# Inverting the recurrence's triangular matrices on 32x32 blocks

## The chip, the cores and the metric

The kernel runs on one core of a Trainium2 chip. The metric is the device time of one execution in microseconds. The engines are TensorE (PE), VectorE (DVE), ScalarE (ACT), GpSimd (POOL) and SyncE (SP), which issues most DMAs. Each runs its own instruction stream in order, and they wait for each other by semaphores.

## What is computed

Two transformer blocks run one after the other over 1024 positions of width 1024 in fp32. The change concerns the second block's recurrent mixer alone: 8 heads of 64, one step per position.

```python
def rwkv7_step(state, inp):
    r_t, w_t, k_t, v_t, a_t, b_t = inp
    sa = jnp.einsum('bhij,bhj->bhi', state, a_t)
    state = state * w_t[:, :, None, :] + sa[..., None] * b_t[:, :, None, :] + v_t[..., None] * k_t[:, :, None, :]
    y = jnp.einsum('bhij,bhj->bhi', state, r_t)
    return state, y
```

The kernel works in chunks of 64 positions. Within a chunk the steps depend on each other through a strictly lower triangular 64x64 matrix M for each head (products of the scaled a and b rows), and the chunk's update needs the inverse of I - M, a lower triangular matrix with ones on its diagonal. Sixteen chunks and eight heads make 128 inverses. Beside the recurrence the second block has a band attention and its projections.

## The kernel before

A "pair-chunk" cp is two neighbouring chunks, 0 to 7 in all; par tells its two chunks apart. Tiles of a pair-chunk hold 8 matrices of 64 columns on each half of the 128 partitions, 16 matrices in 512 columns. The pair-chunks 0 to 3 use data of the first half of the sequence (positions 0 to 511), 4 to 7 of the second.

Order.pre lists a pair-chunk's preparation: pre_x turns v, k and b by matmuls against the identity (L1916); pre_ar, pre_mm and pre_kn are masked products of 64x64 blocks (L1932; masked by DVE at L2808, L2814, L2821); pre_v multiplies KN with v (L1946, evacuated by ACT); pre_i (DVE, L2828 to L2835) and pre_t0 (DVE, L2841) build the first approximations TT and T. Then come five levels. Level l doubles the size of the diagonal blocks that are inverted already, from 2 to 64:

- pre_up: 16 matmuls of 64x64x64 (L1984), AR with T; DVE masks the result with the level's mask lv[l] into X (L2847, two passes of 128x256);
- pre_turn (levels 0 to 3): 16 matmuls (L1999) of TT with X; DVE adds the result to T (L2855, two passes);
- pre_add: 16 matmuls (helper blocks, L1946) of X with TT; DVE adds the result to TT (L2862, two passes).

Order.seq then carries the state through the pair-chunk's two chunks: seq_x (L2011, L2021, L2029), seq_u (L2042), which needs TT of level 4, and seq_z (L2053, L2060). Order.puts_out normalises the outputs (DVE; POOL's seq_gain, L3399 to L3407) and turns them back with seq_out (L2073, DVE L2922). pres, seqs and outs loop over the pair-chunks; pair-chunk cp may start when the outputs of cp - 2 are done, pair-chunk 4 also needs the second half's projections.

The order of all work is written down ahead of time by a planner, Order.flow. It holds a modelled time for each engine and the costs of each step from the function work. Each stream (the gemm tiles as the main one, the pres, seqs, outs, head norms and three lanes of attention bands beside it) offers its next step as soon as its model says that the last one has ended; the gemm fills what is left. So the costs in work decide the order of the instructions on all engines. The eight PSUM banks of P8 are handed out by room; a group of up, turn or add takes two. A gemm product of fp32 takes three matmuls of a 128x512 tile (L1525, L1526, L1527, or L1565 to L1567); DVE and ACT split the weights (L2106, L2967). A band's steps are band_s (L1857; DVE L2699, L2706, L2710; ACT L3271), band_t (transposes at L1511, ACT L3279), band_o (L1878) and band_y (DVE L2716). The gemm stream stops after r1 until pair-chunk 3's operands are read (step ("read", 3), set after pre_kn). After seq_out of pair-chunk 7 and the bands of the first half the gemm fin0 follows, then fin1.

## Time and profile before

| | |
|---|---|
| median of 3 runs | 2421.11 us (2420.31 to 2425.67) |
| the profiled execution | 2418.48 us, of which the span is 2416.6 us |
| mean granted PE clock | 0.972 |
| PE / DVE / ACT / POOL busy | 2277.8 / 1456.7 / 937.6 / 78.7 us |
| instructions in the span | 43216 |

The profile is of one execution. Busy time is the union of an engine's instructions. A matmul in fp32 stands in it as two records, each a weight load (PEld) and a matmul (PE). Matmuls of different tiles of the array overlap, so a group's busy time is shorter than the sum of its matmuls; pages and windows count them with their modelled ends. Times in the timeline are microseconds from the span's start.

### The profile page before, as it was taken

To read this page: it belongs to the slowest core of one execution; us is meant where nothing else is said; L and a number is where in the kernel's file an instruction comes from. 1 tells how busy PE (TensorE), PEld (TensorE's weight loads), DVE (VectorE), ACT (ScalarE), POOL (GpSimd) and SP (SyncE) were. 2 spreads that over 40 slices of the span, in tenths; PEclk is the share of its full clock that TensorE was granted. 3 is DMA by queue.
4 is the path that set the end of the run, shared out by engine and by line. 5 is a ranking of instruction groups with operands and counts; after the bars stand their busy time and mean duration, and the time that the engine had idled before them with its cause. 6 is when DMAs were issued, how large, how long until landed. Compare 5 with 4: busy or idle time off the path is not lost. (4 is left out here: it accounts for less than half of the span.)

```text
span 2416.6 us, 43216 instructions
## 1 busy us (share of the span) xinstructions
PE 2277.8 (94%) x18830; PEld 1848.8 (77%) x18830; DVE 1456.7 (60%) x2456; ACT 937.6 (39%) x1532; POOL 78.7 (3%) x61
## 2 busy tenths in 40 slices
PE   7999988999999999999999999999999998789789
PEld 5777767788888888888878888778777776567667
DVE  5575866565434886777753454646455655767743
ACT  4446432444333443333342433354333232335441
POOL 0000000000000000000000000002000001200000
PEclk9999989999999999999999999989999999799989
DMA  5332252544123232222365534333323113111044
GB/s 179 88 94 66 69 170 71 173 123 129 53 62 119 77 96 83 79 79 86 93 196 164 157 90 135 98 113 110 109 80 107 51 37 97 41 44 44 3 129 150
DMA packets 329349, 238.15 MB, mean 99 GB/s; under 512 B 10948, under 2 KB 288580, under 8 KB 329032
## 3 DMA queue, kind: packets, MB, share of 16 engines
q1 hardware_dynamic: 326424, 229.82, 31.7%
q10 hardware_dynamic: 2736, 5.57, 0.6%
q8 instruction: 148, 2.42, 0.4%
q14 instruction: 41, 0.34, 0.0%
HBM read 202.33 MB, written 33.03 MB: 97 GB/s over the span
## 5 line engine op out<-in xcount | busy, mean ns | idle before, releaser
L1525 PE MATMUL PS<-SR 128*128 128x512 f32 (+2 forms) x1696 | 681.6, 402 | 43.2 <-DVE SR L2106 34.8
L1526 PE MATMUL PS<-SR 128*128 128x512 f32 (+2 forms) x1696 | 659.9, 389 | 0.0
L1527 PE MATMUL PS<-SR 128*128 128x512 f32 (+2 forms) x1696 | 659.7, 389 | 0.0
L2106 DVE TENSOR_TENSOR SR<-SB,SR 128x1024 fp32r<-128x1024 f32 (+1 forms) x240 | 289.1, 1206 | 289.8 <-ACT SR L2967 289.5
L1525 PEld LDWEIGHTS PS<-SR 128*128 128x128 f32 (+1 forms) x1696 | 320.4, 189 | 128.3 <-DVE SR L2106 36.9
L1527 PEld LDWEIGHTS PS<-SR 128*128 128x128 f32 (+1 forms) x1696 | 320.2, 189 | 68.7
L1526 PEld LDWEIGHTS PS<-SR 128*128 128x128 f32 (+1 forms) x1696 | 320.9, 189 | 62.2 <-issue 1.7
L2967 ACT ACTIVATE SR<-SB 128x1024 fp32r<-128x1024 f32 (+1 forms) x240 | 247.5, 1033 | 254.9 <-DMA SB<-in_w_down 116.1
L1546 PE MATMUL PS<-SR 128*128 128x512 f32 x624 | 243.4, 390 | 0.3 <-DVE SR L2232 0.3
L1548 PE MATMUL PS<-SR 128*128 128x512 f32 x624 | 242.8, 389 | 0.0
L1547 PE MATMUL PS<-SR 128*128 128x512 f32 x624 | 242.7, 389 | 0.0
L1546 PEld LDWEIGHTS PS<-SR 128*128 128x128 f32 x624 | 117.1, 188 | 25.1 <-DVE SR L2232 0.7
L1548 PEld LDWEIGHTS PS<-SR 128*128 128x128 f32 x624 | 117.1, 188 | 24.6
L1547 PEld LDWEIGHTS PS<-SR 128*128 128x128 f32 x624 | 117.1, 188 | 24.4 <-issue 0.2
L1511 PE MATMUL PS<-SB 128*128 128x128 f32 (+2 forms) x560 | 87.1, 288 | 31.9 <-DVE SB L2710 13.5
L1511 PEld LDWEIGHTS PS<-SB 128*128 128x128 f32 (+2 forms) x560 | 63.4, 145 | 49.7 <-DVE SB L2710 15.2
L2974 ACT ACTIVATE SB<-PS 128x512 f32<-128x512 f32 (+1 forms) x71 | 39.1, 572 | 151.1 <-PE PS L1527 113.0
L2254 DVE TENSOR_TENSOR SR<-SB,SR 128x1536 fp32r<-128x1536 f32 (+2 forms) x66 | 87.0, 1347 | 0.9 <-ACT SR L3031 0.9
L3031 ACT ACTIVATE SR<-SB 128x1536 fp32r<-128x1536 f32 (+2 forms) x66 | 74.2, 1156 | 20.0 <-DVE SB L2244 18.9
L2142 DVE TENSOR_TENSOR SB<-PS,SB 128x512 f32<-128x512 f32 x48 | 33.2, 691 | 78.7 <-PE PS L1527 78.7
L3279 ACT ACTIVATE SB<-PS 128x640 f32<-128x640 f32 (+4 forms) x64 | 36.4, 569 | 93.7 <-PE PS L1511 93.6
L3065 ACT ACTIVATE SB<-SB 128x1024 f32<-128x1024 f32 x22 | 27.4, 1245 | 116.5 <-DVE SB L2304 116.5
(315 smaller groups left out, 3032.2 us busy)
## 6 DMA issues: line engine op xcount, KB each, us to landing
SB<-in_w_in SPq DMA_DIRECT2D x110, 512.0 KB, 4.0
SB<-in_w_up SPq DMA_DIRECT2D x88, 256.0 KB, 3.3
SB<-in_w_out SPq DMA_DIRECT2D x32, 512.0 KB, 4.2
SB<-in_w_down SPq DMA_DIRECT2D x32, 512.0 KB, 4.1
SB<-in_w_ada SPq DMA_DIRECT2D x12, 1024.0 KB, 5.2
hidden<-SB SPq DMA_DIRECT2D x22, 512.0 KB, 3.4
SB<-hidden SPq DMA_DIRECT2D x43, 256.0 KB, 5.3
asides<-SB SPq DMA_DIRECT2D x36, 256.0 KB, 4.1
```

Of the source, the lines that this page charges most:

```text
L1511: return pe.transpose(out, in_, m.I[0:n, 0:n])
L1525: pe.matmul(out, whi[:, k - k0, :], hi[k], start=(k == 0), stop=False)
L1526: pe.matmul(out, whi[:, k - k0, :], lo[k], start=False, stop=False)
L1527: i = pe.matmul(out, wlo[:, k - k0, :], hi[k], start=False, stop=(k == j.K - 1))
L1546: pe.matmul(out, whi[:, k, :], hi[k], start=first and k == 0, stop=False, skip_group_check=True)
L1547: pe.matmul(out, whi[:, k, :], lo[k], start=False, stop=False, skip_group_check=True)
L1548: x = pe.matmul(out, wlo[:, k, :], hi[k], start=False, stop=(k == 3), skip_group_check=True)
L2106: v.tensor_tensor(m.f32r(a, kn * cn), m.f32(a, kn * cn), m.f32r(a + 1024, kn * cn).bitcast(F32), SUB).then_inc(*on("split.v", p))
L2254: v.tensor_tensor(m.up_unit(m.SR, p, a, 0, b - a), f32_of(p, a, b - a), m.up_unit(m.SR, p, a, 1, b - a).bitcast(F32), SUB).then_inc(*on("u ...
L2967: a.activation(m.f32r(at_ + 1024, kn * cn), m.f32(at_, kn * cn), ACT.Copy).then_inc(*on("split.a", p))
L2974: a.activation(j.dst(t), src, j.func, scale=j.scale).then_inc(*on("gemm.a", "ev", j.name, t))
L3031: a.activation(m.up_unit(m.SR, p, lo, 1, hi - lo), m.up_unit(m.SB, p, lo, 0, hi - lo), ACT.Copy).then_inc(*on("up.a", "hi", p, g))
```

## The change

Only the diagonal blocks of 32x32 are inverted by levels, four in place of five, on compact tiles: TB holds T and TT of all blocks (Tc and TTc, 256 columns each, one set for all pair-chunks), Xc the X. A group of up, turn or add is 32 matmuls of 32x32x32, one on each diagonal 32x32 tile of the array in turn, into one PSUM bank, with one DVE pass of 128x256 behind it. pre_mm computes the diagonal blocks of M and of its transpose (64 matmuls with 64 rows and 32 columns), and DVE masks them and adds the identity in one further pass, which gives T and TT of level -1; pre_i and pre_t0 go. At the end level 4 computes the lower left 32x32 block: up of M's lower left block with T (32 matmuls), a copy to Xc, add with TT (16 matmuls), and copies of the result by DVE (partitions 64 to 95) and ACT (partitions 0 to 31) into the full TT. ACT copies the diagonal blocks into TT (pre_own, four activations), POOL clears TT at the start of each pair-chunk (pre_zero). seq_u waits for the three writers. The costs in work are set anew, the masks become 32 wide, and norms_qk(1) is planned after "qk0".

```diff
-        self.m2, M = f32(X0 + 6656, 640), f32(X0 + 7296, 512)
+        self.m2, TB = f32(X0 + 6656, 352), f32(X0 + 7296, 512)
...
+        self.m0 = v3(m2[:, 128:192], 2).unsqueeze(2).to_broadcast([128, 2, 4, 32])
+        *self.lv, self.I32 = (m2[:, 192 + 32 * i:224 + 32 * i] for i in range(5))
+        self.TB, self.Xc = TB, work(27904, 256)
+        by_kind = TB.rearrange("p (a q j t) -> p a q j t", a=2, q=2, j=4)
+        self.Tc, self.TTc = by_kind[:, :, 0], by_kind[:, :, 1]
...
-        "pre_x": [("pe", 1.0), ("a", 1.0)], "pre_ar": [("pe", 0.95), ("v", 1.38)], "pre_mm": [("pe", 0.48), ("v", 0.84)],
-        "pre_kn": [("pe", 0.95), ("v", 1.38)], "pre_i": [("v", 2.2)], "pre_v": [("pe", 1.9), ("a", 1.2)],
-        "pre_t0": [("v", 0.7)], "pre_up": [("pe", 0.67), ("v", 0.84)], "pre_add": [("pe", 0.95), ("v", 0.84)],
-        "pre_turn": [("pe", 0.67), ("v", 0.84)], "seq_x": [("pe", 1.7), ("v", 0.42)], "seq_u": [("pe", 0.58), ("a", 0.4)],
+        "pre_x": [("pe", 1.0), ("a", 1.0)], "pre_ar": [("pe", 0.95), ("v", 1.38)], "pre_mm": [("pe", 0.6), ("v", 1.55)],
+        "pre_kn": [("pe", 0.95), ("v", 1.38)], "pre_own": [("a", 1.4)], "pre_v": [("pe", 1.9), ("a", 1.2)],
+        "pre_up": [("pe", 0.5), ("v", 0.45)], "pre_add": [("pe", 0.5), ("v", 0.45)], "pre_turn": [("pe", 0.5), ("v", 0.45)], "seq_x": [("pe", 1.7), ("v", 0.42)], "seq_u": [("pe", 0.58), ("a", 0.4)],
...
-                if step[0] not in ("pre_x", "pre_add", "pre_i"):
+                if step[0] not in ("pre_x", "pre_own") and (step[0] != "pre_add" or step[2] == 4):
...
-        yield [("pre_i", cp)]
         yield from one(("pre_v", cp), "pre.a", "nv", cp)
-        yield [("pre_t0", cp)]
-        for l in range(5):
-            yield from one(("pre_up", cp, l), "pre.v", "X", cp, l)
-            if l < 4:
-                yield from one(("pre_turn", cp, l), "pre.v", "T", cp, l)
-            yield from one(("pre_add", cp, l), "pre.v", "TT", cp, l)
+        for l in range(4):
+            yield from single(("pre_up", cp, l), ("pre.v", "X", cp, l))
+            yield from single(("pre_turn", cp, l), ("pre.v", "T", cp, l))
+            yield from single(("pre_add", cp, l), ("pre.v", "TT", cp, l))
+        yield [("pre_own", cp)]
+        yield from single(("pre_up", cp, 4), ("pre.v", "X", cp, 4))
+        yield from single(("pre_add", cp, 4), ("pre.v", "TT", cp, 4), ("pre.a", "far", cp))
         self.done.add(("pre", cp))
...
-                  self.seqs(), self.pres(), self.outs(), self.rotated(1), self.lora_of(1), self.norms_qk(1),
+                  self.seqs(), self.pres(), self.outs(), self.rotated(1), self.lora_of(1), chain(self.after("qk0"), self.norms_qk(1)),
...
+    def corners():
+
+        return [(par, j, h, d, slice(64 * h + 32 * d, 64 * h + 32 * d + 32)) for j in range(4) for par in range(2) for h in range(2)
+                for d in range(2)]
...
+        for q, (lhs, rhs) in enumerate(((sg, aa), (aa, sg))):
+            for j in range(4):
+                for d in range(2):
+                    for par in range(2):
+                        sl = slice(128 * (cp % 4) + 64 * par + 32 * d, 128 * (cp % 4) + 64 * par + 32 * d + 32)
+                        for a in range(2):
+                            to = 64 * (par ^ a) + 32 * d
+                            x = pe.matmul(bank(got[par][0])[to:to + 32, 128 * q + 32 * j:128 * q + 32 * j + 32], lhs[j][half(a), sl],
+                                          rhs[j][half(a), sl], start=True, stop=True)
...
+    def pre_up(cp, l, b, free):
+        AR = m.per[cp % 2]["AR"]
+        w.wait_ge(*at("pre.v", "ar", cp, 1))
+        w.wait_ge(*(at("pre.v", "T", cp, l - 1) if l else at("pre.v", "T", cp)))
+        out = corner(b, free)
+        for par, j, h, d, ps in corners():
+            d, to = (1 - d, slice(64 * h + 32 - 32 * d, 64 * h + 64 - 32 * d)) if l == 4 else (d, ps)
+            c = 512 * par + 64 * j + 32 * d
+            x = pe.matmul(out(to, par, j), AR[ps, c:c + 32], m.Tc[ps, par, j], start=True, stop=True)
         x.then_inc(*on("pre.pe", "up", cp, l))
...
+    def pre_turn(cp, l, b, free):
+        w.wait_ge(*at("pre.v", "X", cp, l))
+        w.wait_ge(*at("pre.v", "TT", cp, l - 1))
+        out = corner(b, free)
+        for par, j, h, d, ps in corners():
+            x = pe.matmul(out(ps, par, j), m.TTc[ps, par, j], Xc(ps, par, j), start=True, stop=True)
         x.then_inc(*on("pre.pe", "turn", cp, l))
+
+    def pre_add(cp, l, b, free):
+        w.wait_ge(*at("pre.v", "X", cp, l))
+        w.wait_ge(*at("pre.v", "TT", cp, l - 1))
+        out = corner(b, free)
+        for par, j, h, d, ps in corners():
+            if l < 4 or d:
+                x = pe.matmul(out(slice(64 * h, 64 * h + 32) if l == 4 else ps, par, j), Xc(ps, par, j), m.TTc[ps, par, j], start=True,
+                              stop=True)
+        x.then_inc(*on("pre.pe", "add", cp, l))
...
-        w.wait_ge(*at("pre.v", "TT", cp, 4, 1))
+        w.wait_ge(*at("pre.v", "TT", cp, 4))
+        w.wait_ge(*at("pre.a", "far", cp))
+        w.wait_ge(*at("pre.a", "own", cp))
...
+        if cp >= 1:
+            w.wait_ge(*at("pre.a", "own", cp - 1))
         for a in range(2):
-            v.tensor_tensor(heads(m.per[cp % 2]["M"], a), h4(bank(got[a][0])[:, 0:256]), bc(m.m0), MUL).then_inc(
-                *on("pre.v", "mm", cp, a))
+            v.tensor_tensor(m.TB[:, 256 * a:256 * a + 256].rearrange("p (q j t) -> p q j t", q=2, j=4),
+                            bank(got[a][0])[:, 0:256].rearrange("p (q j t) -> p q j t", q=2, j=4), m.m0, MUL).then_inc(*on("pre.v", "mm", cp, a))
+        w.wait_ge(*at("pre.v", "mm", cp, 1))
+        v.tensor_tensor(v3(m.TB, 16), v3(m.TB, 16), m.I32.unsqueeze(1).to_broadcast([128, 16, 32]), ADD).then_inc(*on("pre.v", "T", cp))
+        S.also("pre.v", "TT", cp, -1)
...
         w.wait_ge(*at("pre.pe", "up", cp, l))
-        w.wait_ge(*(at("pre.pe", "add", cp, l - 1) if l else at("pre.pe", "v", cp)))
-        for f in range(2):
-            v.tensor_tensor(side(m.per[cp % 2]["KN"][:, 512:1024], f), side4(bank(got[f][0])),
-                            m.lv[l].unsqueeze(1).unsqueeze(1).to_broadcast([128, 2, 2, 64]), MUL).then_inc(*on("pre.v", "X", cp, l, f))
-
-    def pre_turn(cp, l, got):
+        w.wait_ge(*(at("pre.pe", "add", cp, l - 1) if l else at("pre.pe", "mm", cp)))
+        if l < 4:
+            v.tensor_tensor(h8(m.Xc), h8(bank(b)[:, 0:256]), m.lv[l].unsqueeze(1).to_broadcast([128, 8, 32]), MUL).then_inc(
+                *on("pre.v", "X", cp, l))
+        else:
+            v.tensor_copy(m.Xc, bank(b)[:, 0:256]).then_inc(*on("pre.v", "X", cp, l))
...
+        w.wait_ge(*(at("pre.v", "T", cp, l - 1) if l else at("pre.v", "T", cp)))
+        v.tensor_tensor(m.Tc, corner(b), m.Tc, ADD).then_inc(*on("pre.v", "T", cp, l))
...
+        if l < 4:
+            v.tensor_tensor(m.TTc, corner(b), m.TTc, ADD).then_inc(*on("pre.v", "TT", cp, l))
+        else:
+            w.wait_ge(*at("pre.g", "zero", cp))
+            v.tensor_copy(h8(m.per[cp % 2]["TT"])[64:96, :, 32:64], h8(bank(b)[:, 0:256])[64:96]).then_inc(*on("pre.v", "TT", cp, l))
...
+    def pre_own(cp):
+        w.wait_ge(*at("pre.v", "TT", cp, 3))
+        w.wait_ge(*at("pre.g", "zero", cp))
+        TT = m.per[cp % 2]["TT"].rearrange("p (a j t) -> p a j t", a=2, j=4)
+        for h in range(2):
+            for d in range(2):
+                ps = slice(64 * h + 32 * d, 64 * h + 32 * d + 32)
+                i = a.activation(TT[ps, :, :, 32 * d:32 * d + 32], m.TTc[ps], ACT.Copy)
+        i.then_inc(*on("pre.a", "own", cp))
+
+    def pre_add(cp, l, b, free):
+        if l == 4:
+            w.wait_ge(*at("pre.pe", "add", cp, 4))
+            w.wait_ge(*at("pre.g", "zero", cp))
+            a.activation(h8(m.per[cp % 2]["TT"])[0:32, :, 32:64], h8(bank(b)[:, 0:256])[0:32], ACT.Copy).then_inc(*on("pre.a", "far", cp))
...
+    def pre_zero(cp):
+        if cp > 1:
+            w.wait_ge(*at("seq.v", "yr", cp - 2))
+            w.wait_ge(*at("seq.pe", "y", cp - 2, 1))
...
+        g.memset(m.per[cp % 2]["TT"], 0.0).then_inc(*on("pre.g", "zero", cp))
```

## Rows read from the trace of the kernel before

**Rows 1.** The page, part 1: busy us, share of the span, instructions.
```profile
PE 2277.8 (94%) x18830; PEld 1848.8 (77%) x18830; DVE 1456.7 (60%) x2456; ACT 937.6 (39%) x1532; POOL 78.7 (3%) x61
```

**Rows 2.** Windows: stretch, length, busy (count) PE, PEld, DVE, ACT, POOL; PE clock, DMA share, GB/s.
```profile
1700.00:1911.50 211.50, 210.68 (x3089) 164.31 (x3087) 114.51 (x220) 67.47 (x100) 10.24 (x8) 0.99 0.30 91
1911.50:1937.00 25.50, 18.64 (x740) 16.54 (x739) 14.39 (x38) 3.38 (x8) 0.00 (x0) 1.00 0.09 25
...
2040.00:2080.00 40.00, 18.77 (x88) 12.44 (x92) 28.59 (x57) 15.14 (x35) 17.54 (x11) 0.56 0.37 125
2080.00:2290.00 210.00, 181.93 (x4664) 146.02 (x4658) 148.64 (x424) 87.90 (x199) 14.15 (x12) 0.96 0.08 27
2290.00:2318.00 28.00, 11.59 (x95) 7.85 (x92) 18.59 (x40) 16.83 (x29) 4.46 (x4) 0.69 0.25 63
```

**Rows 3.** Groups by line: operands, count | busy us, mean ns | idle before, releaser.
```profile
L1946 PEld LDWEIGHTS PS<-SB 64*64 64x64 f32 x1792 | 56.7, 136 | 15.8 <-issue 9.1 <-DVE SB L2847 3.5 <-DVE SB L2821 2.5
L2862 DVE TENSOR_TENSOR SB<-PS,SB 128x256 f32<-128x256 f32 x80 | 30.1, 419 | 25.9 <-PE PS L1946 25.6
L2847 DVE TENSOR_TENSOR SB<-PS,SB 128x256 f32<-128x256 f32 x80 | 29.9, 416 | 11.3 <-PE PS L1984 11.3
L2855 DVE TENSOR_TENSOR SB<-PS,SB 128x256 f32<-128x256 f32 x64 | 24.1, 418 | 21.0 <-PE PS L1999 21.0
L2832 DVE TENSOR_TENSOR SB<-SB 64x128 f32<-64x128 f32 x32 | 7.8, 283 | 0.2
L2841 DVE TENSOR_TENSOR SB<-SB 128x512 f32<-128x512 f32 x8 | 6.4, 798 | 0.0
L2835 DVE TENSOR_TENSOR SB<-SB 128x512 f32<-128x512 f32 x8 | 5.5, 692 | 0.3
L2828 DVE TENSOR_TENSOR SB<-SB 128x256 f32<-128x256 f32 x8 | 3.4, 419 | 0.0
```

**Rows 4.** Timeline: start us, us, engine line operation, count; groups within the gemm stream.
```profile
1745.00 1.01 PEld L1946 LDWEIGHTS PS<-SB 64*64 64x64 f32 x32 [0.36 <-issue]
...
1746.08 0.50 PE L1525 MATMUL PS<-SR 128*128 128x512 f32 x1
...
1747.66 0.56 PEld L1984 LDWEIGHTS PS<-SB 64*64 64x64 f32 x32 [0.36 <-issue]
...
1748.29 0.50 PE L1842 MATMUL PS<-SR 36*128 36x512 f32 x1
```

**Rows 5.** Timeline: one level without cover, from 1914 us.
```profile
1914.24 0.69 PE L1984 MATMUL PS<-SB 64*64 64x64 f32 x32 [0.88 <-DVE SB L2855]
1915.01 0.76 DVE L2847 TENSOR_TENSOR SB<-PS,SB 128x256 f32<-128x256 f32 x2 [0.16 <-PE PS L1984]
...
1915.82 0.69 PE L1999 MATMUL PS<-SB 64*64 64x64 f32 x32 [0.89 <-DVE SB L2847]
...
1917.40 0.69 PE L1984 MATMUL PS<-SB 64*64 64x64 f32 x32
```

**Rows 6.** Groups on two tiles: 128 columns (group by line, timeline), and one bank.
```profile
L1672 PE MATMUL PS<-SB 128*64 128x128 f32 x240 | 17.4, 289 | 0.0
...
320.96 1.09 PE L1672 MATMUL PS<-SB 128*64 128x128 f32 x16
...
1924.15 0.54 PEld L2011 LDWEIGHTS PS<-SB 64*64 64x64 f32 x16
```

**Rows 7.** Chain of waits from 2150 to 2230: shares of its 80 us by line.
```profile
by line: PE PS L1946 10.6%; PE PS L1857 10.1%; PE PS L1878 8.3%; DVE SB L2710 7.7%; PE PS L1511 7.0%; issue 6.8%; DVE SB L2699 5.5%; PE PS L1999 3.9%; PE PS L1984 3.7%; DVE SB L2847 2.5%; DVE SB L2862 2.5%; PE PS L1916 2.4%; DVE SB L2855 1.
```

**Rows 8.** Groups by line: the nearest rows for ACT's and POOL's new steps.
```profile
L3342 ACT ACTIVATE SB<-PS 128x256 f32<-128x256 f32 x16 | 6.1, 384 | 56.9 <-PE PS L2042 56.9
...
L3404 POOL TENSOR_TENSOR SB<-SB 128x512 f32<-128x512 f32 x8 | 8.7, 1093 | 0.0
```

**Rows 9.** Timeline: pre_v and the first up of pair-chunk 6.
```profile
2191.81 2.08 PE L1946 MATMUL PS<-SB 64*64 64x64 f32 x64 [0.71 <-DVE SB L2821]
...
2196.59 0.69 PE L1984 MATMUL PS<-SB 64*64 64x64 f32 x32 [0.76 <-DVE SB L2841]
```

## What the change does to the time, predicted

> **What bounds the kernel now.** I read the page first, then the windows of the last 700 us, then single stretches of the timeline and of the chain of waits. The page shows TensorE (PE) at 94% and VectorE (DVE) at 60% of the span [rows 1], so an edit pays where PE has less to do or stops waiting. All the code that changes runs between 1700 and 2290 us. The windows split that time into three stages with different limits [rows 2].
>
> Stage A, 1700 to 2040: the four pair-chunks of the first half are prepared between gemm tiles. PE is full (210.68 of 211.5 us), so here only PE time counts, apart from 1911.5 to 1937. There the gemm stream has run out until pair-chunk 3 has been read, and PE works 18.64 of 25.5 us: 6.9 us of idling.
>
> Stage B, 2040 to 2080, PE clock 0.56: projection preparation and a transfer. No edited step runs in it, and I cost it at nothing.
>
> Stage C, 2080 to 2318: pair-chunks 4 to 7 beside the attention bands. PE works 181.93 of 210 us up to 2290 and 11.59 of 28 after, DVE 148.64 and 18.59. Neither is full. Each level of the inverse alternates PE, DVE, PE, DVE, and the last output of pair-chunk 7 opens the final gemm. The chain of waits from 2150 to 2230 goes mostly through PE, 10.6% of it through L1946 alone, the rest of the inverse through L1984 3.7%, L1999 3.9%, and DVE's L2847 and L2862 2.5% each [rows 7].
>
> **The price of a group of small matmuls.** The trace shows each fp32 matmul as two records, weights plus matmul. A group of up or turn has 16 matmuls, 32 records, spread over all four 64x64 tiles of the array; an add (L1946) has as many, but its order leaves only two tiles alternating. Weight loads take 0.56 us in the up group and 1.01 us in the add [rows 4]. Less one load of 0.136 us [rows 3], over 31 steps, that is 13.7 to 13.9 ns and 28.4 ns per record: 55 to 57 ns per record and tile both times. So it is the tile that sets the pace. From its start to the next gemm matmul the up group takes 1747.66 to 1748.29, 0.63 us, and the add 1745.00 to 1746.08, 1.08 us: 31 steps and a fixed 0.20 us.
>
> How does the tile's time depend on the moving columns? A group of 16 records with 128 columns on two tiles takes 1.09 us [rows 6]; less one matmul of 0.289 us, over 15 steps, 53 ns, or 107 ns per record and tile. From 107 at 128 columns and 57 at 64 a line gives about 32 ns at 32 columns. No row has 32 columns: the bounds are 28 (half of 57) and 57 (no gain). I take 31.6, on the line. The new groups of up, turn and add go round four diagonal tiles, so 7.9 ns per record (bounds 7 and 13.9).
>
> **Part by part, per pair-chunk, eight of them.**
> PE: up and turn become 32 matmuls of 32 columns, 64 records: 63 x 7.9 ns + 0.20 = 0.70 us against 0.63, nine times, +0.6. The first four adds cost 0.70 against 1.08, -1.5; the last add (32 records on two tiles, 31 x 15.8 ns + 0.20) 0.69, -0.4. The masked product pre_mm goes from 32 to 128 records over eight tiles; between 3.9 ns (tile) and 7.9 ns I take 6, so 0.96 against 0.63, +0.3. Sum: -1.0 us. The groups stay as many as they were.
> DVE: 28 passes of 128x256 become 14, two of which are now copies. The old ones cost 30.1 + 29.9 + 24.1 = 84.1 us for all eight [rows 3]; half goes, -42 us. pre_i (L2828, L2832, L2835) and pre_t0 (L2841) go: 3.4 + 7.8 + 5.5 + 6.4 = 23.1 us. pre_mm keeps its two passes and gains one of 128x512 at 0.69 us, +5.5. Sum -60 us, 7.4 per pair-chunk. The copy of 32 partitions costs what a full pass costs, as pieces on 64 partitions cost 283 ns for 128 columns; bounds 0.1 and 0.42.
> ACT gains four copies of the diagonal blocks and one of the far block, 256 elements per partition each; nearest row 384 ns [rows 8]: 1.9 us. They stand after level 3, beside up, X and add of the last level (about 2.3 us), and in front of Us in ACT's queue. ACT is busy 87.90 of 210 us in stage C [rows 2]; cover gone, the price is up to 1.9 us per pair-chunk, bound 0 to 8 us in stage C.
> POOL gains a memset of TT. Bounds 0.3 and 1.4 us (a 128x512 pass takes 1.09 [rows 8]). It waits for the output of two pair-chunks before; behind it in the queue is the next gain step, which waits for DVE later still. TT is needed only after level 3, some 20 us on: nothing on the path. The load g_load beside it does not move.
> New waits: DVE's pre_mm waits for ACT's own of the pair-chunk before, as TB is shared, and behind it queue pre_kn and the bands' passes; own is done long before, since seq_u already needed it. seq_u waits for three events in place of one; the last level ends about when it did. The order by planner is cast anew by the shorter costs, which also lets a group take one PSUM bank in place of two; norms_qk(1) is only held behind its first half. I give these nothing, -5 to +5 us.
>
> **The sum.** Stage A: PE -1.0 x 4 = -3.9 us. The 6.9 us of idling end when pair-chunk 3 is read. A level without cover takes 1914.24 to 1915.82 to 1917.40, 3.16 us [rows 5]; each half is 0.77 from the group's start to DVE's, 0.76 of DVE and 0.05 to the next group. The new level takes 2 x (0.84 + 0.42 + 0.05), 2.6 us. Three pair-chunks of five levels are 8 us shorter bare, and pre_i and pre_t0 lie no longer ahead of the first up; that is more than 6.9, so I take all of it. Stage A: -10.8 us.
> Stage C: the chain of 80 us has 8.5 us in L1946; 0.38 of 1.08 goes, -3.0. L2847, L2862 and L2855 hold some 4.8 us, of which 0.34 of 0.76 goes, -2.2; up and turn +0.6. That is -4.6 in 80 us, -13 over 230. The front: after pre_v (2191.81 + 2.08) the first up waits until 2196.59, the last 0.76 us of it for pre_t0 [rows 9], the rest covered by bands; between 0.8 and 2.7 per pair-chunk I take 2, -8. pre_mm: +0.5 per pair-chunk, +2. Stage C: -19 us.
> Together -30 us. The profiled execution has a span of 2416.6 and a time of 2418.48 us; its forecast is 2388.5. The median of the runs lies 2.6 us above it, so the forecast for the median is 2391 us.
>
> **A page against it.** The rows show the tile's time following the columns from 128 to 64 [rows 4, 6]. The Trainium skill, TensorEngine Tiling (Array Packing), Instruction Overhead, says that every matmul bears about 60 cycles, so that 60 columns cost no less than one, and warns not to take a tiling factor from a dimension that is already small. By it the records would double at the old pace, which is the second rival below; by the line they do not. No row here is below 64 columns, so the trace leaves it open.
>
> **Rivals.**
> 1. The stage C gain isn't there: the bands' own chain (score, maximum, exponential, turn, output) sets the end, and shorter levels only open gaps. For it: bands hold PE L1857, L1878 and L1511, each as large on the chain as L1946. Against it: the inverse is in the chain all along, and seq_out of pair-chunk 7 precedes the final gemm while bands are still left to run beside it. Then stage A's 10.8 and at most a third of stage C's: 2404 to 2414, about 2409.
> 2. The other side: the pace stays per record. A nanosecond more per record costs PE 0.95 us per pair-chunk: 3.8 us in stage A, and 2.5 in stage C at two thirds on the path, 6.3 in all. The gain of 30 is used up at 7.9 + 4.8 = 12.7 ns. At 13.9 ns, the shortest pace of the rows, it is +8 us: 2429 (2421 to 2437). For it: no row shows less. Against it: two tiles and four tiles give the same time per tile.
> 3. Four row groups writing into one PSUM bank take turns. Old groups use two banks, new ones one. Price 31.6 ns per record: +24 x 6.3, about 2540. Against it: L2011 writes one bank from two tiles, 16 records in 0.54 us, 27 ns apart, the pace of two free tiles [rows 6]. In a sentence for itself: the same page of the Trainium skill, Gotcha 1: PSUM Pressure, says different row tiles can't access one bank at the same time; the trace does not agree for two tiles.
> 4. It does more: bands move wholly behind the last pair-chunk, beside the final gemm, and fill the idling after 2290, where PE waits 16.4 of 28 us [rows 2]. Up to 15 us further: 2372 (2365 to 2378).
>
> **How the numbers follow.** Forecast (2378 to 2404) 0.58; rival 1 0.18; rival 2 0.12, of which 0.05 near break-even; rival 3 0.05; rival 4 0.07. The measurement tells 0.2%, 4.8 us, from no change. Faster: 0.58 + 0.07 + 0.17 of rival 1, 0.82. Within: 0.05 + 0.01. Slower: 0.07 + 0.05. The range takes in rival 1 and half of rival 4: 2372 to 2416, leaving out rivals 2 and 3 and the low tail.
>
> **What the profile after would show.** Groups of 64 records of 32 columns with weight loads spanning about 0.6 us (0.9 or more: rival 2; 2 us: rival 3). DVE some 60 us less busy. No idling stretch near 1911. Pair-chunks 4 to 7 in about 47 us each in place of 52. The final gemm's start about 30 us earlier. Wrong would be: PE as busy in stage A as before with more records; ACT's copies just ahead of seq_u; or an unchanged distance from the first pre_x of pair-chunk 4 to the final gemm.

## The result, and the profile after

The changed kernel takes 2451.9 us (median of four runs, 2445.99 to 2457.59) against 2420.71 us before in the same comparison: 1.0125 times as long, 95% interval 1.0095 to 1.0155. It is 31 us slower where the prediction had it 30 us faster, and lies outside the range. The profiled execution took 2445.99 us, its span is 2444.2 us.

The page of the changed kernel, part 1 (against [rows 1]):

```profile
span 2444.2 us, 51324 instructions
...
PE 2289.9 (94%) x22926; PEld 1855.6 (76%) x22926; DVE 1404.1 (57%) x2296; ACT 952.6 (39%) x1572; POOL 82.3 (3%) x69
...
q8 instruction: 180, 2.95, 0.5%
```

DVE lost 53 us, near the 60 forecast, and PE gained 12 where it should have lost 8. The count of instructions rose from 43216 to 51324, by 8108. The last line is the queue that brings instructions: 180 packets of 16 KB. The same line of the page of the kernel before is

```profile
q8 instruction: 148, 2.42, 0.4%
```

and 32 packets more for 8108 instructions more are one for about 256.

The windows by stage of the changed kernel (the columns are those of [rows 2]):

```profile
1911.50:1937.00 25.50, 22.18 (x795) 17.84 (x795) 10.98 (x23) 6.42 (x13) 0.00 (x0) 1.00 0.20 57
1937.00:2083.70 146.70, 121.51 (x1748) 91.48 (x1751) 81.01 (x148) 48.37 (x85) 30.40 (x22) 0.88 0.22 71
2083.70:2339.00 255.30, 199.47 (x6758) 159.71 (x6755) 137.70 (x371) 108.46 (x239) 18.85 (x18) 0.88 0.10 30
2339.00:2444.20 105.20, 101.75 (x515) 81.63 (x515) 41.45 (x57) 26.97 (x37) 0.00 (x0) 0.98 0.46 144
```

And the same of the kernel before, cut at its own events:

```profile
1937.00:2079.60 142.60, 121.27 (x1218) 91.79 (x1217) 85.24 (x164) 46.82 (x79) 29.99 (x20) 0.85 0.23 73
2079.60:2317.70 238.10, 193.62 (x4762) 153.97 (x4761) 167.37 (x462) 104.75 (x228) 18.60 (x16) 0.93 0.10 31
2317.70:2416.60 98.90, 95.70 (x464) 78.03 (x464) 37.46 (x45) 23.10 (x29) 0.00 (x0) 0.98 0.49 153
```

The edges are the first pre_x of pair-chunk 4 (2079.6 before, 2083.7 after) and the first matmul of the final gemm (2317.7, 2339.0). So stages A and B end 4.1 us later, stage C is 17.2 us longer (255.3 against 238.1), and the final gemm takes 6.3 us more: 27.6 us of span. In stage C the matmul records rose from 4762 to 6758, and the mean granted clock fell from 0.93 to 0.88. Of its two levels, 1.2 and 2.4 GHz, the lower (0.5) then holds for 0.12 / 0.5 = 24% of the stage, before for 14%.

The chain of waits names what is new. Its shares by line in stage C, before and then after:

```profile
by line: PE PS L1857 10.6%; PE PS L1878 9.4%; PE PS L1511 8.7%; DVE SB L2699 7.4%; PE PS L1946 6.6%; issue 6.0%; DVE SB L2710 5.1%; PE PS L1999 3.4%; PE PS L1916 2.8%; PE PS L1984 2.8%; ACT SB L3279 2.7%; PE PS L1932 2.2%; DVE SB L2847 2.2%
```

```profile
by line: issue 15.1%; PE PS L1865 11.4%; PE PS L1886 11.2%; PE PS L1519 11.1%; PE PS L2033 5.9%; PE PS L2016 5.4%; PE PS L1924 4.0%; PE PS L2024 3.6%; PE PS L1940 2.9%; ACT SB L3303 2.8%; DVE SB L2735 2.8%; PE PS L1954 2.4%; PE PS L1994 2.2
```

"issue" is time in which an engine waits for nothing that the profile shows. It is 14 us of the chain before (6.0% of 238.1) and 39 us after (15.1% of 255.3), more than any line of work. The weight loads' timeline of the changed kernel shows how one such piece looks (start, length, instruction, and in brackets the idle time ahead):

```profile
2088.21 1.11 PEld L1994 LDWEIGHTS PS<-SB 64*32 64x32 f32 x121
2091.13 0.15 PEld L1994 LDWEIGHTS PS<-SB 64*32 64x32 f32 x7 [1.81 <-issue]
...
2109.27 0.62 PEld L2016 LDWEIGHTS PS<-SB 32*32 32x32 f32 x59
2111.61 0.14 PEld L2016 LDWEIGHTS PS<-SB 32*32 32x32 f32 x4 [1.72 <-issue]
...
2176.98 0.61 PEld L2016 LDWEIGHTS PS<-SB 32*32 32x32 f32 x58
2179.46 0.19 PEld L2016 LDWEIGHTS PS<-SB 32*32 32x32 f32 x5 [1.86 <-issue]
```

A group of matmuls that wait for nothing stops in its midst, for 1.7 to 1.9 us. I counted as a pause every distance of over 0.42 us from the start of one weight load to the start of the next inside a group, with no wait on the later one, leaving out the band scores of L1865, which show such distances in both kernels. Before there is one, of 0.46 us. After there are 30, together 41 us (38 us of it idle): 8.9 in stages A and B, 32.5 in stage C. Each ends 2.3 to 2.9 us after an instruction packet started.

The pauses lie on a grid. From one to the next the trace has exactly 128 weight loads nine times, otherwise 1 to 11 fewer than a multiple of 128. A load and its matmul are two instructions, and some waits stand on TensorE as instructions of their own. Counted with these, all 29 distances are multiples of 256 instructions to within one: one packet.

This gives the theories for the experiments. F: TensorE passes its instructions faster than they are fetched. O: the planner's new costs made a worse order. Neither was among the prediction's rivals.

### The profile page after: what moved, and what is told of

Same layout as the page of the kernel before. It is cut to its first block and busy times, and to the rows that moved or that the text cites. A ratio compares the mean times of both kernels' runs of the same rounds, so it can differ in the third digit from the quotient of the medians.

```text
span 2444.2 us, 51324 instructions
## 1 busy us (share of the span) xinstructions
PE 2289.9 (94%) x22926; PEld 1855.6 (76%) x22926; DVE 1404.1 (57%) x2296; ACT 952.6 (39%) x1572; POOL 82.3 (3%) x69
## 5 line engine op out<-in xcount | busy, mean ns | idle before, releaser
L3424 POOL TENSOR_TENSOR SB<-SB 128x512 f32<-128x512 f32 x8 | 16.5, 2063 | 1673.5 <-DVE SB L2778 1673.5
```

## The experiments

The kernel before was timed beside each, with medians of 2420.1, 2421.4, 2418.1 and 2422.0 us in the four sets.

### Twice the instructions in the kernel before

```diff
-            x = pe.matmul(... 128 * par + 64 * jl:128 * par + 64 * jl + 64], both(r["AR"])(c, 0, j)[ps, :],
-                          head(r["KN"])(c, 0, j)[ps, :], start=True, stop=True)
+            x = pe.matmul(... at0:at0 + 32], both(r["AR"])(c, 0, j)[ps, :],
+                          head(r["KN"])(c, 0, j)[ps, 32 * s:32 * s + 32], start=True, stop=True)
```

> The kernel before, with each 64-column matmul of pre_mm, up, turn and add split into two of 32 columns that load the same weights; the results, steps, waits, passes and the planner's order stay those of before. Records of matmuls per pair-chunk in these groups rise from 480 to 960, near the 992 of the changed kernel. Theory F (the changed kernel loses its gain because TensorE runs short of instructions): the groups' tile time grows by little (five adds by 0.12 us, ten others by 0.07 us: 1.3 us per pair-chunk, at most 10 us), and beyond that come stalls in the middle of groups with no wait there, some 1.5 us each: 2435 to 2470 us, about 2450. Theory O (the planner's new order and costs lose it): the order is that of before, so at most the tile time is lost: 2421 to 2431 us, and no stalls in the middle of groups.

Measured: 2504.3 us, ratio 1.0341 (1.0322 to 1.0361). Slower than either theory had it, and not by pauses: there are five, 4.8 us in all. The time is PE's, 2358.4 us busy against 2277.8. Split groups cost twice their old time:

```profile
1740.40 1.02 PEld L1997 LDWEIGHTS PS<-SB 64*64 64x64 f32 x64
...
1743.05 1.02 PEld L2021 LDWEIGHTS PS<-SB 64*64 64x64 f32 x64 [0.36 <-issue]
```

64 records in 1.02 us, less a load of 0.138 and over 63 steps, are 14.0 ns each, what they cost with 64 moving columns [rows 4]. Half the columns saved nothing; the weights are still 64 wide (below). The nine groups of up and turn pay 32 x 14 ns more, the five adds 32 x 28.2, pre_mm some 0.5 us: 9 us per pair-chunk, 72 in all, of the 84 us that were lost.

On F it says one thing: the count alone doesn't make the pauses. This kernel has 50896 instructions and 178 packets, nearly those of the changed one, and five pauses against 30. Its fastest stretch of 128 weight loads takes 2.13 us, that of the changed kernel 1.22, that of the kernel before 2.52. That the slower groups leave the fetch time is argued from these, not tested by itself.

### Half the instructions in the changed kernel

```diff
-        return [(par, j, h, d, slice(64 * h + 32 * d, 64 * h + 32 * d + 32)) for j in range(4) for
+        return [(par, j, h, d, slice(64 * h + 32 * d, 64 * h + 32 * d + 32)) for j in (0, 2) for
...
-            x = pe.matmul(out(to, par, j), AR[ps, c:c + 32], m.Tc[ps, par, j], start=True, stop=True)
+            x = pe.matmul(out(to, par, j), AR[ps, c:c + 32], m.Tc[ps, par, j:j + 2], start=True, stop=True)
```

> The changed kernel with half as many matmuls in up, turn, add and pre_mm, each with 64 moving columns in place of 32: it writes the columns of two neighbouring blocks with the weights of the first, so the second block's result is not its own. Waits, passes of VectorE, the order and the bytes moved stay those of the changed kernel; the tile time of a group stays within 0.1 us; the records per pair-chunk fall from 992 to 496. Theory F: the stalls in the middle of groups are gone and the gain that was predicted appears: 2385 to 2410 us, about 2395. Theory O: as the order is unchanged, the time stays at 2440 to 2455 us.

Measured: 2383.5 us, ratio 0.9846 (0.9831 to 0.9861), a little below F's range and far from O's. It is 68 us less than the changed kernel with its waits, passes and order (it leaves out the products of every second block, which get those of their neighbour's weights). One pause is left (2.2 us). Stage C, cut at the same events, and its chain:

```profile
2067.60:2276.00 208.40, 173.24 (x4775) 135.55 (x4775) 136.86 (x371) 108.46 (x239) 18.93 (x18) 0.96 0.12 36
```

```profile
by line: PE PS L1865 12.9%; PE PS L1886 11.1%; PE PS L1519 10.3%; issue 7.4%; ACT SB L3303 4.6%; PE PS L1940 4.1%; DVE SB L2735 3.8%; PE PS L2033 3.7%; PE PS L1924 3.4%; PE PS L1954 2.9%; PE PS L2016 2.8%; DVE SB L2746 2.5%; DVE SR L2953 2.
```

"issue" is back at 15 us (7.4% of 208.4), the granted clock at 0.96, and the stage takes 208 us where the changed kernel takes 255. O can't explain this, as the order is the same. The groups themselves became shorter too: from the first load's start to the last one's end an up, turn or add takes 0.49 us against 0.64, pre_mm 0.70 against 1.11. That is 2.5 us per pair-chunk, so of the 68 us up to 20 can be array time; how much of it is on the path I didn't measure. The fillers below hold the array time still.

### Transposed blocks: the same inverse with fewer instructions

```diff
+    def flip(cp, l):
+        w.wait_ge(*(at("pre.v", "T", cp, l) if l >= 0 else at("pre.v", "T", cp)))
+        v.transpose(m.TB[:, 256:512], m.TB[:, 0:256]).then_inc(*on("pre.v", "TT", cp, l))
...
-            yield from single(("pre_add", cp, l), ("pre.v", "TT", cp, l))
+            yield [("pre_flip", cp, l)]
```

> The changed kernel, with TT of levels -1 to 3 made by VectorE: one transposition of 32x32 blocks of T (128x256, fp32) in place of the add group and its pass in PSUM, and pre_mm computes M alone (64 records, not 128). Records per pair-chunk fall from 992 to 672. The transposition is not on the chain from level to level, since only the next turn needs it. Theory F: most stalls go, since few groups are left that follow each other without a gap, and TensorE has some 2.8 us per pair-chunk less to do besides: 2370 to 2405 us, about 2385. Theory O: the lighter work gives at most those 2.8 us four times in the first half and some 10 us in the second: about 2430 us (2420 to 2440).

Measured: 2389.1 us, ratio 0.9869 (0.9854 to 0.9884), near F's 2385 and not O's 2430. 46152 instructions, eight pauses of 6.8 us in all. The transposition takes DVE what the pass in PSUM took it:

```profile
L2854 DVE STREAM_TRANSPOSE SB<-SB 128x256 f32<-128x256 f32 x40 | 17.6, 439 | 0.6
```

### The old costs, the changed kernel's instructions

```diff
-"pre_mm": [("pe", 0.6), ("v", 1.55)], "pre_up": [("pe", 0.5), ("v", 0.45)], ...
+"pre_mm": [("pe", 0.48), ("v", 0.84)], "pre_up": [("pe", 0.67), ("v", 0.84)], "pre_add": [("pe", 0.95), ("v", 0.84)], ...
```

> The changed kernel planned with the costs that the kernel before gave to pre_mm, up, turn and add; nothing else. The instructions are the same, in an order nearer to that of before. Theory O: 2395 to 2415 us. Theory F: the same number of instructions still runs in the same groups, so the stalls stay, shifted at most: 2440 to 2460 us.

Measured: 2435.8 us, ratio 1.0066 (1.0048 to 1.0084). Both were off: 16 us come back, fewer than O had and more than F. Pauses fall from 41 to 31 us, which is 10 of the 16. That the order acts by how close it sets the groups to each other is argued from this, not shown.

### Small matmuls by themselves

```diff
+        for i in range(160):
+            for h in range(4):
+                ps = slice(32 * h, 32 * h + 32)
+                pe.matmul(bank(1)[ps, 32 * (i % 8):32 * (i % 8) + 32], m.TTc[ps, 0, 0], m.Tc[ps, 0, 0], start=True, stop=True)
+        large(16)
...                                # 512 of 64x64x64 on four tiles, then 256 on two
```

> The changed kernel with runs of matmuls set behind its end, where no other engine works, each between some large matmuls: 640 matmuls of 32x32x32 round four diagonal tiles (2560 instructions), 512 of 64x64x64 round four tiles (2048), 256 on two tiles (1024), then 64 and 1536 empty instructions. What the profile before its end shows is as before; the time itself is of no interest. Theory F: instructions come in blocks of 256, and a block can't come faster than one in some 2.5 us; so the 32-column run has pauses every 128 records, no wait near them, and takes about 25 us (10 blocks) where the pace of its tiles would make 1280 x 7.9 ns = 10 us; the four-tile 64-column run takes about 20 us where its tiles would make 14 us; the two-tile run takes its 28 ns per record, 14.5 us, without pauses. Rival R (the pauses come from what else runs in the kernel, such as transfers that compete, or memory traffic): no pauses here, 10, 14 and 14.5 us.

Measured in one execution, weight loads behind the kernel's end (L2124: 32x32 tiles; L2129: 64x64, four tiles; L2134: 64x64, two tiles):

```profile
2461.90 1.53 PEld L2124 LDWEIGHTS PS<-SB 32*32 32x32 f32 x168
2465.77 1.80 PEld L2124 LDWEIGHTS PS<-SB 32*32 32x32 f32 x128 [2.35 <-issue]
2469.26 1.80 PEld L2124 LDWEIGHTS PS<-SB 32*32 32x32 f32 x128 [1.69 <-issue]
2472.75 1.80 PEld L2124 LDWEIGHTS PS<-SB 32*32 32x32 f32 x128 [1.69 <-issue]
...
2520.60 1.96 PEld L2129 LDWEIGHTS PS<-SB 64*64 64x64 f32 x128 [2.06 <-issue]
2524.34 1.96 PEld L2129 LDWEIGHTS PS<-SB 64*64 64x64 f32 x128 [1.79 <-issue]
...
2533.30 15.01 PEld L2134 LDWEIGHTS PS<-SB 64*64 64x64 f32 x512
```

F: runs of exactly 128 records with a pause between, one packet for each (8 packets from 2466 to 2495), with nothing else at work. A block comes every 3.5 to 4.0 us, longer than the 2.5 expected, so the first run took 34 us, not 25, and the second 28, not 20. The two-tile run needs 29 ns per record, 3.7 us per block, and doesn't pause. It isn't a matter of 32x32 tiles: 64x64 ones on four tiles pause alike. The first 168 records passed without a pause, so a short group alone meets none; blocks in quick succession do. The empty instructions behind these runs left no mark in the trace.

In the first run the granted clock was 0.50 from 2465.7 on, with PE busy for 16.3 of 30.1 us, and the 128 records of a block then took 1.80 us; in the second it was 0.94, with 17.9 busy of 28. Stage C of the changed kernel has 0.88 and that of the paired one 0.96. So the lower level came together with pauses in one run and not in the other; that pauses bring it isn't shown, and a run without any had 0.70 (below).

The Trainium skill, Runtime: NRT & Kernel Launch, Instruction fetch mechanics, says that instructions are fetched in blocks of 16 KiB, 256 instructions, and that crossing into the next is mostly hidden, since the engine passes instructions more slowly than they are filled in. The first agrees with the packets here; the second doesn't, for TensorE with small matmuls, and the measurement decides.

### Fillers

```diff
+    def fill(n):
+        for i in range(n):
+            pe.nop()              # second kernel: pe.wait_ge(*at("gates.v", "m0"))
```

> The kernel with paired columns (half the matmuls in pre_mm, up, turn and add; the second block of a pair is not its own result) with as many empty instructions set behind each group on TensorE as it has saved: 128 after pre_mm, 64 after each up, turn and add, 32 after the last add. The last matmul still releases VectorE before them. Theory F: the count of instructions is what costs, so the pauses come back at about the places of the changed kernel: 2430 to 2460 us, about 2445, against 2383.5 without them. Rival R: what costs is something about small matmuls themselves (their tiles, weights or PSUM writes), so empty instructions cost only their own issue: 2384 to 2400 us.

> The kernel with paired columns, with waits as filler (the empty instructions of the run before didn't reach the program: its trace has as many instruction packets as the one without them). Behind each group on TensorE stand waits on a semaphore that was reached over a thousand microseconds earlier: 128 behind pre_mm, 64 behind each up, turn and add, 32 behind the last add, as many as the changed kernel has instructions more there. The matmuls, order and results stay. Theory F: the instruction packets rise from 149 to some 180 and pauses of 0.5 to 2.5 us come back every 256 instructions, some 30 to 40 us in all, plus the waits' own issue, at 6.4 ns each (the pace at which the run of 32-column matmuls at the end passed its instructions between pauses) 6.6 us per pair-chunk, of which the first half pays all four times and the second two thirds: 44 us. Together 2440 to 2480 us, about 2460. Rival R (small matmuls are the cause, not the count): no pauses in the middle of groups, and only the issue: 2384 to 2430 us.

Neither tests the count. With empty instructions the trace has 43388 instructions and 149 packets, as the paired kernel without them: they are not in the program, and 2382.2 us merely repeats its time. With waits it is 2869.8 us: 486 us for 7936 waits, 61 ns each, ten times what I had assumed. The trace has 47356 instructions and 165 packets, so only 3968 instructions and 16 packets more: two waits stand in each, and these instructions follow each other every 106 ns, 53 ns per wait. A wait that was fulfilled long ago isn't free on PE, and 256 such instructions take 27 us, which hides any fetching.

### The same array time in small and in large matmuls

```diff
+                    pe.matmul(out(ps, par, j), m.I[ps, ps], m.I[ps, ps], start=True, stop=True)   # 32 of them
...
+            pe.matmul(bank(b)[:, 128 * i:128 * i + 128], m.I, m.I, start=True, stop=True)          # or 2 of these
```

> The kernel with transposed blocks and the old costs (2382.8 us), with 32 more matmuls of 32x32x32 in front of each up and turn of levels 0 to 3, on the same tiles and into the same bank, where the group then overwrites them. That is 64 records (128 instructions) more per group, 0.50 us of the tiles' time, in eight groups per pair-chunk, 4.0 us; the first half pays 16 us, the second two thirds to all, 11 to 16 us: 2410 to 2415 us from array time alone. The planner doesn't know of them. Theory F: each such group is 256 instructions, a whole block, so nearly every one meets a pause of 1.5 to 2.5 us: 64 groups, of which half or more pause, 50 to 130 us on top: 2460 to 2540 us, about 2490. Rival R (array time is what counts): 2405 to 2420 us.

> The same kernel, with two matmuls of 128x128 with 128 moving columns in front of each up and turn of levels 0 to 3, in place of the 32 small ones: 4 records of 0.11 us, 0.44 us, and 8 instructions more per group, and a change from full array to tiles in each. Array time is within 0.1 us of that with the small ones. Theory F and rival R alike: 2383 plus 14 us in the first half and 9 to 14 in the second: 2405 to 2415 us. The difference between this run and the one before is the price of 120 instructions per group: F 50 to 130 us, R 0 to 7 us.

Measured: 2485.2 us with the small ones (ratio 1.0262, 1.0244 to 1.0280), 2407.0 with the large ones (0.9938, 0.9924 to 0.9953), from a base of 2382.8: F's range for the first, and the 2405 to 2415 forecast for the second. 78 us lie between them, for 120 instructions in each of 64 groups: 10 ns per instruction. The array time is near the same, as the loads of one group without a pause show, small and then large (extra matmuls, then the first load of the group proper):

```profile
1735.38 0.63 PEld L1973 LDWEIGHTS PS<-SB 32*32 32x32 f32 x63 [0.25 <-issue]
...
1735.92 0.63 PEld L2022 LDWEIGHTS PS<-SB 32*32 32x32 f32 x63
```

```profile
1737.20 0.52 PEld L1970 LDWEIGHTS PS<-SB 128*128 128x128 f32 x4 [0.24 <-issue]
1737.84 0.64 PEld L2019 LDWEIGHTS PS<-SB 32*32 32x32 f32 x64
```

The small ones take 0.54 us there, the large ones 0.64. Pauses: 39 of 52 us in all against 2 of 1.4 us, so 51 of the 78 us; the mean granted clock of the profiled executions, 0.957 against 0.972, goes the same way, and I didn't split the rest. The chain from pair-chunk 4 to the final gemm, small and then large:

```profile
by line: PE PS L1864 14.2%; issue 12.7%; PE PS L1885 9.6%; PE PS L1518 9.2%; PE PS L1973 8.5%; PE PS L2022 4.3%; PE PS L2031 4.0%; DVE SB L2741 3.5%; PE PS L1923 3.0%; PE PS L1953 2.9%; ACT SB L3315 2.4%; PE PS L1939 2.0%; DVE SR L2965 1.7%
```

```profile
by line: PE PS L1864 13.8%; PE PS L1518 9.0%; PE PS L1885 8.8%; DVE SB L2738 6.4%; PE PS L1970 5.9%; PE PS L1953 3.6%; PE PS L2019 3.6%; PE PS L1923 3.5%; PE PS L2028 3.3%; issue 3.3%; ACT SB L3312 3.1%; PE PS L1939 2.5%; DVE SB L2749 2.5%;
```

This settles what the paired kernel left open: with no more array time, the additional instructions in dense groups make the difference.

### What sets the time of a record

> The changed kernel with seven runs of 48 matmuls (96 records) behind its end, each on one tile of the array, for the time of a record by the tile's weights (rows x columns) and the moving columns; the time of the whole is of no interest. Prediction's line (the moving columns alone set it): 32x32 weights with 32, 64 and 128 moving columns 32, 57 and 107 ns per record; 64x64 weights with 32, 64 and 128 moving columns 32, 57 and 107 ns; 64x32 weights with 32 moving columns 32 ns. Rival W (the larger of the weights' columns and the moving columns sets it, as the split kernel suggests): the same but for 64x64 weights with 32 moving columns, 55 to 57 ns.

The weight loads of six of the seven runs in one execution, one tile each, in the order of the text above (the third is left out):

```profile
2455.23 3.28 PEld L2122 LDWEIGHTS PS<-SB 32*32 32x32 f32 x96
...
2463.71 6.06 PEld L2122 LDWEIGHTS PS<-SB 32*32 32x32 f32 x96
...
2497.10 5.92 PEld L2122 LDWEIGHTS PS<-SB 64*64 64x64 f32 x96
...
2508.15 5.67 PEld L2122 LDWEIGHTS PS<-SB 64*64 64x64 f32 x96
...
2517.66 10.45 PEld L2122 LDWEIGHTS PS<-SB 64*64 64x64 f32 x96
...
2532.05 3.11 PEld L2122 LDWEIGHTS PS<-SB 64*32 64x32 f32 x96
```

Less one load and over 95 steps: 32.9 ns (weights 32 wide, 32 moving columns), 62 (32, 64), 60 (64, 32), 58 (64, 64), 109 (64, 128) and 31.6 ns (64 rows, 32 wide, 32 moving). Rival W holds: the larger of the weights' width and the moving columns sets it. The granted clock was 0.93, 0.88 and 0.95 in the first, second and fourth run and 1.00 in the last three, so 62 and 60 are a little high. The third run, with 32 and 128 columns, had 0.70 with PE busy all of its 14.7 us, and its pace says nothing.

The Trainium skill, TensorEngine Tiling (Array Packing), Instruction Overhead, which the prediction cites, lets 32 columns cost what 60 do. That agrees where the weights are 64 wide (60 ns against 58), and not where they are 32 wide (32.9 against 62).

### The order of the kernel with transposed blocks

Only costs (in one, one stream) differ from the kernel with transposed blocks, whose up and turn have 0.50 us for TensorE and 0.45 for VectorE. In order: 0.70 and 0.45, with pre_mm at 0.70 and 1.4 and the transposition at 0.45; the old costs; those with `self.norms_qk(1)` in place of `chain(self.after("qk0"), self.norms_qk(1))`; those with VectorE at 1.2 for up and turn; and the old costs of up and turn, with pre_mm and the transposition as in the first.

> The kernel with transposed blocks planned with what its profile shows for the groups: 0.70 us for up, turn and add on TensorE in place of 0.50, pre_mm 0.70 and 1.4, the transposition 0.45. Only the order changes. Theory O' (costs that understate the groups hurt, since the planner then puts groups too close together): 2375 to 2387 us. Theory N (without the stalls the order matters little): 2386 to 2394 us.

> The kernel with transposed blocks planned with the costs of the kernel before for pre_mm, up, turn and add (and 0.84 for the transposition). Only the order changes. The changed kernel gained 16 us from these costs, of which its profile puts 10 in fewer stalls. Theory O': wider spacing helps here too, 2375 to 2387 us. Theory N: 2386 to 2398 us, since too high costs put up to 0.4 us per step of gemm work between steps of the chain in the second half.

> The kernel with transposed blocks and the old costs (2382.8 us), with norms_qk(1) planned as before the change, not held behind the first half. Only the order of the second half's norms moves. If the hold matters: 2 to 10 us slower, 2385 to 2393 us, as the norms' groups then stand among the first pair-chunks. If it doesn't: 2380 to 2386 us.

> The kernel with transposed blocks and the old costs, with 1.2 us in place of 0.84 for VectorE's part of up and turn, so that the planner sets the levels still further apart. Theory O' (wider spacing helps): 2374 to 2380 us. Theory N (the old costs are about wide enough; more only lengthens the levels of the second half, 8 steps by up to 0.36 us four times, 11 us): 2383 to 2395 us.

> The kernel with transposed blocks, with the old costs for up and turn (0.67 and 0.84), but 0.70 and 1.4 us for pre_mm and 0.45 for the transposition, as its profile shows. If the wider spacing of the levels is what gained 6 us: 2379 to 2386 us. If the lower cost of pre_mm did: 2387 to 2394 us.

Measured: 2394.3, 2382.8, 2385.7, 2398.6 and 2384.9 us, against 2389.1. The first lies at the slow edge of what its two theories had, the fourth beyond it. Costs true to the profile are no better (+5.2), the old ones are (-6.3), and those of up and turn alone do it (2384.9). 1.2 us in place of 0.84 is too wide (+15.8 from 2382.8). The 95% intervals of kernels 5 to 6 us apart overlap a little here (0.9854 to 0.9884 at 2389.1, 0.9830 to 0.9862 at 2382.8), so the signs of these small steps are likely, not certain. The hold of norms_qk(1) can't be told from nothing: 2.9 us, while that run's interval (0.9835 to 0.9897) takes in both. Why 0.84 for a pass that takes 0.42 orders best is open; pauses (6.8 us at 0.45, 6.4 at 0.84) don't explain it.

The kernel with transposed blocks and the old costs beats both: 2382.8 us, ratio 0.9846 (0.9830 to 0.9862), 39 us less than before and 69 less than the changed one.

## Why the prediction was wrong

The step that failed is the one that it gave half a sentence: "The groups stay as many as they were." They do, but the instructions in them doubled, from 480 matmul records per pair-chunk to 992, and nothing stood for it in the sum. Rival 2 counted the records, but as time of the array's tiles; none of the rivals had TensorE out of instructions. It was worth 68 us by the paired kernel, of which up to 20 are shorter groups, and at 10 ns per instruction, as the small and large fillers have it, 8108 would make 81. The view to look at was there: the page's row of the instruction queue and its count, beside the shortest time in which PE goes through 128 weight loads, 2.52 us between 1700 us and the end. 128 records at the forecast 7.9 ns are 1.0 us, under half of the 2.3 to 2.9 us from a packet's start to the first load behind it, as the changed kernel's trace has it.

Point by point:
- Pace, rivals 2 and 3. The number was right, its reason half right. Two groups back to back in the changed kernel take from 1740.94 to 1742.18, 0.62 us each against 0.70 forecast (weight loads of the changed kernel, the timeline's view; the last row is the first load behind them):

```profile
1740.94 0.62 PEld L2033 LDWEIGHTS PS<-SB 32*32 32x32 f32 x63 [0.36 <-issue]
...
1741.48 0.66 PEld L2016 LDWEIGHTS PS<-SB 32*32 32x32 f32 x63
1742.18 0.97 PEld L1831 LDWEIGHTS PS<-SB 128*128 128x128 f32 x8
```

Four row groups in one bank cost nothing. But the line through 64 and 128 moving columns [rows 4, 6] rests on weights 64 wide in both rows, and can't be carried below 64 with them: 32 moving columns are only cheap because the weights shrank as well. The split kernel, with 32 columns on weights still 64 wide, is 84 us slower than the kernel before. (The add's 28.4 ns in the prediction is 28.2 by its own terms; nothing hangs on it.)
- pre_mm: 6 ns per record forecast, 8.4 measured (121 in 1.11 us, less one load), so eight tiles are no faster than four: 0.3 us more each.
- DVE: passes as forecast. The identity pass took 692 ns, the copies of 32 partitions 422, the upper bound. ACT: 414 ns for each copy of pre_own and 369 for the far block, 2.0 us per pair-chunk against 1.9. POOL's memset: 0.57 us, within 0.3 and 1.4.
- Stage A: -10.8 forecast, +4.1 measured. 1911.5 to 1937 has 3.3 us of idling left of 6.9, 3.3 more than forecast, pauses add 8.9 and pre_mm 1.2. That makes +2.6. But 1.4 us of the pause that ends at 1937.6 lie within that idling and are counted twice, so some 3 us stay unexplained.
- Stage C: -19 forecast, +17.2 measured. The chain's "issue" grew by 24 us, and the granted clock fell from 0.93 to 0.88; how the two share the loss I didn't measure. Pair-chunks 5 to 7 start 42, 60 and 59 us after the one before, where some 47 were named; the kernel before had 40, 57 and 49, the paired one 36, 44 and 45. With the pauses gone the stage is 29.7 us shorter than before (208.4). Up to 10 of them are the shorter groups of four pair-chunks, so the mechanism that was forecast is there, at about its estimate or above.
- Stage B and the end: B cost nothing, as said (its first pass on DVE starts 3.6 us later than before, its last 4.3). Costed at nothing too was the final gemm, which takes 6.3 us longer in the changed kernel and 6.5 in the paired one (2276.0 to 2381.4), as more bands are left to run beside it (16 weight loads of band_s and 80 of band_o, against none and 60 before). The bands move as rival 4 had it, but they cost time there and save none.
- Order, given -5 to +5: 16 us in the changed kernel, 10 of them pauses, and 6 in the kernel with transposed blocks, where there are few.

In all, -30 forecast, and -37 in the paired kernel, which has the change with half its instructions. Without its shorter groups that would be -17 to -37, which takes in the forecast; no run has it more exactly.

## What to carry to other kernels

Cutting matmuls into smaller tiles keeps the array's time and multiplies the instructions; count them, and compare the time that TensorE takes for 256 with the 3.5 to 4.0 us that a block took here. Small groups spread among long matmuls are nearly free of it (8.9 us of pauses in stages A and B), groups close to each other are not (32.5 in stage C). If small tiles are wanted, take the instructions out elsewhere: a transposition on VectorE in place of a second product was worth 63 us here, with the product's array time in it.

## What was not expected of the hardware

- When TensorE runs out of instructions, a block of 256 takes 3.5 to 4.0 us, 14 to 16 ns per instruction, 27 to 31 ns per record.
- A record's time on a tile goes by the larger of weights' width and moving columns: 60 ns at 64 and 32, 32 ns at 32 and 32.
- Waits on TensorE for a semaphore reached long ago cost 61 ns each, in instructions of two waits that follow each other every 106 ns.
- While it paused for instructions in a run by itself, TensorE fell to the lower clock (0.50) in one of two such runs; in another run by itself it had 0.70 while busy without a break.
